# A hybrid decoder layer: storing the split weights of the first down projection for the second, a new order of gate sums and prologue, and another ending

## The chip, the core and the metric

The kernel runs on one core of a Trainium2 chip. The metric is the device time in microseconds (us) of the whole program; lower is better. The core has five engines that run their own instruction streams and meet at semaphores: TensorE (PE, matmuls), VectorE (DVE), ScalarE (ACT), GpSimd (POOL) and SyncE (SP), which here only issues DMA transfers.

## The reference

The input `x` has 2048 tokens of 1024 channels, fp32. There is one layer, and then a final RMSNorm:

```python
mod = (silu(c) @ ada_w[l] + ada_b[l])[:, None, :]
sh1, sc1, g1, sh2, sc2, g2 = jnp.split(mod, 6, axis=-1)
h = rmsnorm(x, norm1_g[l]) * (1 + sc1) + sh1
x = x + g1 * hybrid_mixer(h, ...)      # w_in, a chunked scan, a spatial gate, w_out
h = rmsnorm(x, norm2_g[l]) * (1 + sc2) + sh2
x = x + g2 * conv_gated_ffn(h, ...)
return rmsnorm(x, final_g)

def conv_gated_ffn(h, w_up, conv_w, conv_b, w_down):
    gate, val = jnp.split(h @ w_up, 2, axis=-1)
    gate = causal_dwconv(gate, conv_w, conv_b)
    return (jax.nn.silu(gate) * val) @ w_down
```

The mixer projects to z, x/B/C, dt, u and v; x/B/C go through a causal convolution of width 4 and a chunked scan (16 heads of 64, state 128); u and v through a spatial gating per chunk of 128 tokens; both results, normalized, through `w_out`. The inner width of the FFN is 2816.

## The kernel before, in words

**Tiles and precision.** The tokens are cut into NB = 4 blocks of 512. Every fp32 product is made from halves: an operand is split into a rounded high part and the remainder (fp32r), and three of the four products of halves are summed in PSUM. One **unit** is a weight tile of 128 x 512 with the 12 matmuls (128x512) that use it. PSUM has eight banks: `main[0..3]`, which collect the projections, and `aux[0..3]` (in the profile mostly `pair`).

**Stages.** `mixer(0)`, `mixer(1)`, `ffn(0)` for blocks 0 and 1, `mixer(2)`, `mixer(3)`, `ffn(1)` for blocks 2 and 3. A mixer has 104 units: 0 to 23 for x/B/C (XBC), 24 to 55 for u and v (UV), 56 to 71 for z (Z), 72 to 103 for the output projection (OUT). An FFN takes two blocks at once and makes seven products instead of eight from sums and differences of quarters: 154 units of the up projection, then 77 of the down projection (7 products of KG = 11, in the order P1, P2, P6, P7, P4, P5, P3). In the profiled execution unit 0 of mixer 0 starts at 46.3 us, mixer 1 at 427.0, the first up at 786.3, the first down at 1221.1, mixer 2 at 1446.7, mixer 3 at 1787.7, the second up at 2128.8, the second down at 2561.4; in mixer 0 unit 88 starts at 373.9.

**Weights.** They pass through a ring of RING = 4 slots. SyncE loads a raw tile (`load`, 256 KB), ScalarE makes its high half (`split`, line 811), GpSimd the low one (`low`, line 696), TensorE uses it. Mixer 0 also stores both halves (`store_split`, 512 KB) in `w_split_scratch`, and a split of mixer 0 waits until the halves that stood in its slot before are stored. Mixers 1 to 3 load the halves ready made (line 401): such a load needs a free slot, and no split. Of the 77 weight tiles of down, 35 (`PRE_J`) are loaded, split and stored in mixers 2 and 3 by `pre_load`, `pre_high`, `pre_low`, `pre_store`, and the second down loads these ready made; the other 42 it splits itself, and the first down splits all 77. The up weights' sums are made in mixer 1 and the first up at the units T_AT (`t_load`, `t_store`).

**SyncE** issues in program order. `beside(b, n)` puts other transfers ahead of unit n's load, each with its own waits: the stores of `h_scratch` by mixer 1, the `x2` loads from n = 89 on, the `xnew` loads at n = 79 to 82, and the gate loads at the units `GATE_AT`. While it waits, no later load is issued.

**adaLN.** `mod` needs c_act @ ada_w. For norm 1, `mod_direct` makes the first `ADA_PE` rows' share as matmuls of one column, and VectorE sums the others (`ada_sum`), after which `mod_column` reduces them on TensorE; `mod_column(1)` does so for norm 2 after unit 15. For the two gates, eight blocks `gate_sums(0..7)` on VectorE use 16 loads `gate_load` (two at each of the eight `GATE_AT` units; the loads at index i wait for the sums of block i-1), and eight matmuls (`gate_mm`, after OUT unit 11, that is unit 83) reduce them; SyncE waits for them before the first `x2` load.

**Transposes.** TensorE transposes normalized tokens (`h_transpose`), `y` in two groups (after OUT units 1 and 7) and, for the next block, `h` in two groups (after OUT units 17 and 23), through `aux`; ScalarE takes the high halves out (`yT_hi`), VectorE the low ones.

**Ending.** In the last products of down, P5 and P3 (units 55 to 76), the right-hand halves of the sum are finished: GpSimd multiplies `y_half` by the gate (`final_step`), VectorE adds it to `x_half` (`add_y`, line 1813), ScalarE squares for the last norm, GpSimd multiplies by the gain (`final_gain`), ScalarE scales, SyncE stores. In the same units VectorE makes `a_lo`, the low half of down's left operand (line 1606), for the coming unit.

## Time and profile before

| | us |
|---|---|
| median of 3 runs of the kernel before | 2797.31 |
| lowest and highest of them | 2796.26 and 2800.71 |
| the profiled execution | 2801.3 |
| its span in the trace | 2799.5 |
| TensorE busy in it | 2713.2 (97%) |
| VectorE busy | 1836.2 (66%) |
| GpSimd busy | 1100.9 (39%) |
| ScalarE busy | 994.8 (36%) |
| DMA, mean over the span | 222 GB/s |

The span is cut into stages by the starts of their first units, given above. A windows row has, for a stretch, its length, the busy time and the number of instructions of each engine, the granted clock of TensorE as a share of the full one, the busy share of the 16 DMA engines and what they moved. A timeline row has the start and the length of a run of like instructions, and in brackets how long the engine stood idle before it and what released it.

### The profile page before, as it was taken

Reading aid. Unit: us, or ns where it says so; the run is one execution under the profiler, and the core shown is the slowest. Engines: PE = TensorE matmul, PEld = TensorE weight load, DVE = VectorE, ACT = ScalarE, POOL = GpSimd, SP = SyncE. Lnnn points to the kernel's source line nnn. Section 1 sums busy time; section 2 is a strip of 40 time slices with the busy share of each in tenths; the row PEclk is TensorE's granted clock in tenths of the full one; section 3 lists DMA queues with packets and bytes.
Section 4 is the critical chain, followed back from the end, with each engine's and each line's share of the span. In section 5 each row is a group of like instructions: output and inputs, shape, how many; then the busy total and the mean of one; then the engine's idle time right before and its main releaser. Section 6 shows DMA issues by size and latency. Waiting matters only on the chain.

```text
span 2799.5 us, 33836 instructions
## 1 busy us (share of the span) xinstructions
PE 2713.2 (97%) x12427; PEld 2214.5 (79%) x12427; DVE 1836.2 (66%) x2589; ACT 994.8 (36%) x1505; POOL 1100.9 (39%) x737
## 2 busy tenths in 40 slices
PE   6999999899999999999999999999999999999997
PEld 6777877678877888877878788888888788887885
DVE  6787955668377566568786565565746754545767
ACT  2544323331153333344535322152224433334333
POOL 3344430555047777644560110001003554444244
PEclk9999999999999999999999999999999999999998
DMA  9678777999755665583448767586675334347545
GB/s 385 228 256 298 254 267 256 345 351 332 261 183 187 208 220 188 185 288 88 162 150 293 235 214 277 179 283 231 220 254 191 122 115 121 127 126 249 180 158 199
DMA packets 262001, 620.49 MB, mean 222 GB/s; under 512 B 26725, under 2 KB 84553, under 8 KB 257739
## 3 DMA queue, kind: packets, MB, share of 16 engines
q1 hardware_dynamic: 261174, 618.08, 64.5%
q8 instruction: 99, 1.62, 0.2%
q14 instruction: 66, 0.54, 0.1%
q10 hardware_dynamic: 662, 0.24, 0.0%
HBM read 466.57 MB, written 151.66 MB: 221 GB/s over the span
## 4 chain that ended last, share of the span: by engine, by line
PE 75%; DVE 8%; DMA 7%; POOL 3%; issue 3%; SPq 2%; ACT 1%; DVEq 0%; ACTq 0%; POOLq 0%
PE main L1956 29%; PE pair L2226 15%; PE main L2226 14%; PE pair L2246 6%; PE main L2246 4%; DMA w_split_scratch<-w_hl 2%; POOL tb L714 2%; PE pair L2093 1%; DMA tb<-in_ff_up_dram 1%; DVE a_lo L1606 1%; DMA t_up_scratch<-tb 1%; POOL w_hl L703 1%; PE pair L2118 1%; DMA w_hl<-w_split_scratch 1%; DVE stats L1167 1%
## 5 line engine op out<-in xcount | busy, mean ns | idle before, releaser
L703 POOL TENSOR_TENSOR w_hl<-w_raw,w_hl 128x512 fp32r<-128x512 f32 x532 | 764.1, 1441 | 904.8 <-ACT w_hl L818 902.8
L818 ACT ACTIVATE w_hl<-w_raw 128x512 fp32r<-128x512 f32 x532 | 332.2, 630 | 802.7 <-PE main L2226 169.3
L1956 PE MATMUL main<-w_hl,h_hi 128*128 128x512 f32 x1536 | 492.3, 401 | 4.8 <-DMA w_hl<-w_split_scratch 4.3
L1956 PEld LDWEIGHTS main<-w_hl,h_hi 128*128 128x128 f32 x1536 | 283.8, 188 | 78.3 <-issue 14.2
L1956 PE MATMUL main<-w_hl,h_lo 128*128 128x512 f32 x768 | 300.2, 391 | 0.0
L751 POOL TENSOR_TENSOR pre_hl<-pre_raw,pre_hl 128x512 fp32r<-128x512 f32 x35 | 53.0, 1518 | 564.2 <-ACT pre_hl L842 564.2
L714 POOL TENSOR_TENSOR tb<-tb,tb 128x512 f32<-128x512 f32 x132 | 209.8, 1590 | 164.8 <-DMA tb<-in_ff_up_dram 160.1
L1956 PE MATMUL main<-h_hi,w_hl 128*128 128x512 f32 x768 | 250.6, 400 | 8.2 <-DMA w_hl<-w_split_scratch 5.8
L1606 DVE TENSOR_TENSOR a_lo<-g,a_hi 128x512 fp32r<-128x512 f32 x132 | 176.8, 1349 | 103.4 <-ACT a_hi L1071 103.1
L2226 PE MATMUL pair<-s_hi,w_hl 128*128 128x512 f32 x736 | 235.6, 393 | 2.4 <-POOL w_hl L703 2.4
L2246 PE MATMUL main<-w_hl,a_hi 128*128 128x512 f32 x704 | 222.1, 397 | 16.1 <-DVE a_lo L1606 12.9
L2226 PE MATMUL main<-s_hi,w_hl 128*128 128x512 f32 x672 | 215.5, 393 | 1.9 <-DVE s_lo L1599 1.2
L1669 DVE SCALAR_TENSOR_TENSOR c_acc<-c_gate,col_b,c_acc 128x512 f32<-128x512 f32 x176 | 211.5, 1241 | 4.7 <-ACT c_acc L1037 2.4
L1956 PEld LDWEIGHTS main<-h_hi,w_hl 128*128 128x128 f32 x768 | 146.9, 191 | 41.4 <-DMA w_hl<-w_split_scratch 7.5
L2246 PEld LDWEIGHTS main<-w_hl,a_hi 128*128 128x128 f32 x704 | 132.1, 190 | 52.0 <-issue 17.7
L1956 PEld LDWEIGHTS main<-w_hl,h_lo 128*128 128x128 f32 x768 | 144.1, 188 | 31.7
L2226 PEld LDWEIGHTS pair<-s_hi,w_hl 128*128 128x128 f32 x736 | 138.1, 188 | 35.6 <-POOL w_hl L703 3.2
L2246 PE MATMUL pair<-w_hl,a_hi 128*128 128x512 f32 x528 | 163.3, 390 | 1.4 <-DVE a_lo L1606 1.3
L1956 PE MATMUL main<-w_hl,gmT_hi 128*128 128x512 f32 x512 | 158.5, 391 | 2.2 <-ACT stage L899 1.4
L2226 PEld LDWEIGHTS main<-s_hi,w_hl 128*128 128x128 f32 x672 | 126.1, 188 | 33.5 <-issue 2.9
L1956 PE MATMUL main<-h_lo,w_hl 128*128 128x512 f32 x384 | 151.7, 395 | 0.0
L1956 PE MATMUL main<-w_hl,yT_hi 128*128 128x512 f32 x480 | 150.3, 395 | 0.0
(281 smaller groups left out, 5115.8 us busy)
## 6 DMA issues: line engine op xcount, KB each, us to landing
w_hl<-w_split_scratch SPq DMA_DIRECT2D x312, 512.0 KB, 4.4
w_split_scratch<-w_hl SPq DMA_DIRECT2D x104, 512.0 KB, 6.7
w_raw<-t_up_scratch SPq DMA_DIRECT2D x176, 256.0 KB, 2.7
w_raw<-in_ff_up_dram SPq DMA_DIRECT2D x132, 256.0 KB, 3.7
tb<-in_ff_up_dram SPq DMA_DIRECT2D x88, 256.0 KB, 4.7
t_up_scratch<-tb SPq DMA_DIRECT2D x88, 256.0 KB, 5.7
g_scratch<-c_val SPq DMA_DIRECT2D x44, 512.0 KB, 4.0
g<-g_scratch SPq DMA_DIRECT2D x40, 512.0 KB, 7.3
```

The costliest lines, as they stand in the source:

```text
L703: nc.gpsimd.tensor_tensor(w_lo[:, g % RING, :], w_raw[:, g % RING, :], w_hi[:, g % RING, :].bitcast(F32), ALU.subtract).then_inc(w_lo_ok, 1)
L714: nc.gpsimd.tensor_tensor(dst, one, other, how).then_inc(t_add, 1)
L751: nc.gpsimd.tensor_tensor(pre_hl[i % PRE_BUF][:, 1, :], pre_raw[i % 2][:], pre_hl[i % PRE_BUF][:, 0, :].bitcast(F32), ALU.subtract).then_i ...
L818: nc.scalar.activation(w_hi[:, g % RING, :], w_raw[:, g % RING, :], ACT.Copy).then_inc(w_hi_ok, 1)
L1167: last = V.bn_stats(stats[:, s, :], part)
L1606: V.tensor_tensor(a_lo[j % RING][:], full_a, a_hi[j % RING][:].bitcast(F32), ALU.subtract).then_inc(a_lo_ok, 1)
L1669: last = V.scalar_tensor_tensor(out=piece, in0=c_gate[q % 2][:, i, lo:lo + BT], scalar=col_b[:, R_FW + tap * KF + m:R_FW + tap * KF + m + ...
L1956: ins = T.matmul(main[i], a, w, start=first and p == 0, stop=last and p == 2)
L2093: last = T.matmul(aux[2 + h // (NH // 2)][:, o:o + HD], arow[:, h, :], xdt[:, h * HD:(h + 1) * HD], start=True, stop=True)
L2118: last = T.matmul(aux[2 * (t % 2) + h // 4][:, (h % 4) * P:(h % 4 + 1) * P], wsT[:, h, :], v_sb[:, h // 4, t, (h % 4) * P:(h % 4 + 1) * P] ...
L2226: ins = T.matmul(got[:, i, :], w[:, kl, cols], a[:, k, :], start=k == 0 and m == 0, stop=k == KH - 1 and m == 2)
L2246: ins = T.matmul((main, aux)[p % 2][i], a, w[:, s_w, :], start=k == 0 and m == 0, stop=k == KG - 1 and m == 2)
```

## The change

It has five parts.

**Down's halves.** The first down stores the halves of all its 77 tiles (`store_half(j)`, 512 KB each, issued behind the load of unit j + 4, the last four after the loop), its splits wait until the halves of four units before are stored, and mixer 2's first four loads wait for the last of these stores. The second down loads all 77. Nothing is split in mixers 2 and 3: the four `pre_` functions are gone.

**Prologue.** `mod_direct` goes into `main[1]` in two halves; the transposes of `xn` come between them, ahead of those of the parameter rows, which go to `main[0]`. ScalarE scales `xn` before it copies the parameter columns. `mod_columns` takes its base from a sum made once. The count of `mod_col` is one higher everywhere.

**Mixer 0.** `mod_column(1)` moves from after unit 15 to after unit 18. `GATE_AT` changes; `gate_sums(4)` comes after the scaling of v, 5 after `y_ok`, 6 before and 7 after `norm_x`. The gate matmuls move from after unit 83 to after unit 87. The evacuation of OUT's left half stands ahead of the last split of the loop. The second group of `h` transposes comes two units later, and VectorE makes the first four low halves of `h` ahead of the residual.

**Mixer 1.** `T_AT` starts at unit 20, not 16.

**Ending of the second down.** The gate and gain rows and block 3's `x2` are loaded in P4 into the region of `h` (`g2_last`, `fg_last`, `x_last`). The multiplications of GpSimd are made by VectorE (`gate_half`, `gain_left`, `right_scale`); squares are placed anew; ScalarE scales the left halves (`output_end`).

The diff, cut to its core, eight columns of indentation taken off (a line "..." stands where lines are left out):

```diff
-PRE_J = list(range(2 * KG, 3 * KG + 1)) + list(range(5 * KG - 1, ND))
-pre_d = nc.dram_tensor("down_split_scratch", [len(PRE_J), P, 2, W], F32, kind="Internal").ap()
+pre_d = nc.dram_tensor("down_split_scratch", [ND, P, 2, W], F32, kind="Internal").ap()
 gg_d = nc.dram_tensor("g_scratch", [KF, P, FT], F32, kind="Internal").ap()
...
-GATE_AT = (20, 34, 42, 50, 58, 68, 78, 84)
-PRE_OF = {2: range(17), 3: range(17, len(PRE_J))}
-PRE_AT = [22 + 17 * i // 5 for i in range(18)]
-PRE_BUF = 3
-pre_hi_ok, half_sum, sq_ok = sem("pre_hi_ok"), sem("half_sum"), sem("sq_ok")
+GATE_AT = (22, 34, 42, 50, 58, 70, 80, 85)
+half_sum, sq_ok = sem("half_sum"), sem("sq_ok")
 T_OF = (range(0), range(0, 20), range(20, 33))
-T_AT = ((), [16 + 16 * i // 5 for i in range(20)], [18 + 19 * i // 2 for i in range(13)])
+T_AT = ((), [20 + 16 * i // 5 for i in range(20)], [18 + 19 * i // 2 for i in range(13)])
...
+def half_stored(j):
+    return 16 * (MU // RING) + 16 * (j // RING + 1)
...
+PRE_G = {ffn0(NSB - 1) + DOWN + j: j for j in range(ND)}
+def x_of(s, half):
+    return x_last if half and s == NSB - 1 else x_half[half]
...
+                sp.wait_ge(hl_st[n], half_stored(ND - RING + (n + 1) % RING))
             sp.wait_ge(w_used, mix0(b) + n + 1)
...
-        sp.wait_ge(mod_col, 3)
+        sp.wait_ge(mod_col, 4)
...
+        if s == NSB - 1:
+            sp.wait_ge(half_sum, 4 + (0 if half else 2 * NT) + t + 1)
+        sp.dma_start(ov[2 * s + half, t], x_of(s, half)[:, t, :]).then_inc(y_stored, 16)
+    def store_half(j):
+        g = ffn0(0) + DOWN + j
+        sp.wait_ge(w_lo_ok, split_no(g) + 1 + RING)
+        sp.dma_start(pre_d[j], w_hl[:, g % RING, :, :].bitcast(F32)).then_inc(hl_st[g % RING], 16)
...
-            if (p, k) == (P5, 2):
+            if s + 1 == NSB and p == P4 and 3 <= k < 7:
+                if k == 3:
+                    sp.wait_ge(a_lo_ok, s * ND + (P7 + 1) * KG)
+                    sp.dma_start(g2_last[:], gate_d[1:2, :].broadcast_to([P, D])).then_inc(g2y_in, 16)
+                    sp.dma_start(fg_last[:], final_g.unsqueeze(0).broadcast_to([P, D])).then_inc(fg_in, 16)
+                sp.dma_start(x_last[:, k - 3, :], x2_d[2 * s + 1, k - 3]).then_inc(fin2_in, 16)
+            if s + 1 < NSB and (p, k) == (P5, 2):
...
+                if k == 3:
+                    sp.wait_ge(a_lo_ok, s * ND + (P4 + 1) * KG)
...
+            if s == 0 and j >= RING:
+                store_half(j - RING)
...
+        if s == 0:
+            for j in range(ND - RING, ND):
+                store_half(j)
...
-        pool.wait_ge(d_add, s * (12 + NT) + {(0, 0): 2, (1, 0): 8, (1, 1): 10, (0, 1): 12}[half, c])
+        pool.wait_ge(d_add, s * (12 + NT) + {(0, 0): 2, (1, 0): 8, (1, 1): 10}[half, c])
...
-        if b == NB:
-            for i in range(len(PRE_J)):
-                pre_low(i)
...
-        if b == NB:
-            for step in range(8):
-                final_step(s, step)
-            final_gain(s)
...
-    act.wait_ge(col_tr, 2)
-    nc.scalar.activation(col_a[:], aux[0][:, 0:ROWS_A], ACT.Copy).then_inc(col_ok, 1)
-    nc.scalar.activation(col_b[:], aux[0][:, P:P + ROWS_B], ACT.Copy).then_inc(col_ok, 1)
...
         tile = xn01[:, t, :] if t < 2 else xn23[:, t - 2, :]
         nc.scalar.activation(tile, tile, ACT.Copy, scale=rstd[:, t:t + 1]).then_inc(xn_ok, 1)
+    act.wait_ge(col_tr, 2)
+    nc.scalar.activation(col_a[:], main[0][:, 0:ROWS_A], ACT.Copy).then_inc(col_ok, 1)
+    nc.scalar.activation(col_b[:], main[0][:, P:P + ROWS_B], ACT.Copy).then_inc(col_ok, 1)
...
+        if RING <= g - ffn0(0) - DOWN <= ND:
+            act.wait_ge(hl_st[g % RING], half_stored(g - ffn0(0) - DOWN - RING))
...
-    def half1_scale():
...
+    def left_scale(half, done):
+        for t in range(NT):
+            xx = x_of(NSB - 1, half)[:, t, 0:W]
+            nc.scalar.activation(xx, xx, ACT.Copy, scale=rstd[:, 4 * half + t:4 * half + t + 1]).then_inc(done, 1)
+    def output_end():
         act.wait_ge(r1_ok, 1)
+        left_scale(1, y2_ok)
         for t in range(NT):
-            act.wait_ge(fg_mul, 5 + t // 2)
-            nc.scalar.activation(x_half[1][:, t, :], x_half[1][:, t, :], ACT.Copy, scale=rstd[:, 4 + t:5 + t]
-                                 ).then_inc(y2_ok, 1)
-    def half0_end():
-        for t in range(NT):
-            squares(0, 1, 4 + t + 1, (t,))
+            squares(0, 1, 4 + NT + t + 1, (t,))
         act.wait_ge(xr_ok, NSB + 1)
-        for t in range(NT):
-            nc.scalar.activation(x_half[0][:, t, 0:W], x_half[0][:, t, 0:W], ACT.Copy, scale=rstd[:, t:t + 1]
-                                 ).then_inc(y20_ok, 1)
+        left_scale(0, y20_ok)
...
+                if j == 0 and n == n0 + 2 * KD + LEAD - 1:
+                    evac_to_stage(G_OUT, S_OUT, n0 + 2 * KD - 1, ACT.Copy)
...
-                if b % 2 == 0 and j == 1 and n in (n0 + LEAD + 1, n0 + LEAD + 7):
+                if b % 2 == 0 and j == 1 and n in (n0 + LEAD + 1, n0 + LEAD + 9):
...
-            if j == 0:
-                evac_to_stage(G_OUT, S_OUT, n0 + 2 * KD - 1, ACT.Copy)
...
+            if s == NSB - 1 and p == P5 and k in (6, 7):
+                squares(1, 0, 1, (2 * k - 12, 2 * k - 11))
             if s == NSB - 1 and p == P5 and k in (9, 10):
-                squares(0, 0, 1, (2 * k - 18, 2 * k - 17))
-            if s == NSB - 1 and p == P3 and k in (6, 7):
-                squares(1, 0, 2, (2 * k - 12, 2 * k - 11))
-            if (s, p, k) == (NSB - 1, P3, 8):
-                squares(1, 1, 3)
+                squares(0, 0, 2, (2 * k - 18, 2 * k - 17))
+            if s == NSB - 1 and p == P3 and k in (7, 8):
+                squares(1, 1, 3, (2 * k - 14, 2 * k - 13))
...
+        dve.wait_ge(mod_col, done + 1)
+        cols = two_parts(mod_c, 2 * n * KD, ks)
+        link(V.tensor_tensor(cols, two_parts(bank, 0, ks), base, ALU.add))
         V.scalar_tensor_tensor(out=cols[:, 1, :], in0=cols[:, 1, :], scalar=1.0,
...
+    dve.wait_ge(mod_col, 1)
+    link(V.tensor_tensor(mod_c[:, 0:2 * KD], main[1][:, 0:2 * KD], col_b[:, R_AB:R_AB + 2 * KD], ALU.add))
...
-        mod_columns(0, slice(4 * half, 4 * half + 4), (main[3 - 2 * half], main[2]), R_N1, 1 + half)
-    dve.sem_inc(evacuated, 4)
-    full_at = [acc[:, 0, :], acc[:, 1, :]]
-    h_lows(0, (0, 1), aux, full_at)
+        ks = slice(4 * half, 4 * half + 4)
+        mod_columns(0, ks, main[3 - half], two_parts(mod_c, 0, ks), R_N1, 1 + half)
+        dve.sem_inc(evacuated, 2)
+        if half == 0:
+            h_lows(0, (0, 1), aux, full_at)
...
-                mod_columns(1, slice(0, KD), (aux[0],), R_N2, 3)
+                mod_columns(1, slice(0, KD), aux[0], two_parts(col_b, R_AB + 2 * KD, slice(0, KD)), R_N2, 3)
...
-            if b == 0:
+            if b == 0 and cc < NT - 1:
...
+        if b == 0:
+            gate_sums(NT)
...
-        if b == 0:
-            gate_sums(5)
...
-            gate_sums(6)
+            gate_sums(5)
...
-            gate_sums(7)
+            gate_sums(6)
...
+            gate_sums(7)
...
+        if b == 0:
+            h_lows(b + 1, range(4), aux, [acc[:, 0, :], acc[:, 1, :]])
...
-            h_lows(b + 1, range(KD), aux, [acc[:, 0, :], acc[:, 1, :]])
+            h_lows(b + 1, range(0 if b else 4, KD), aux, [acc[:, 0, :], acc[:, 1, :]])
...
-            if (p, k) == (P5, 7):
-                dve.wait_ge(pool_fin, s * 6 + 2)
-                add_y(s, 0, 0)
...
+                if (p, k) == (P5, 1):
+                    gate_half(s, 0, 0, 2)
+                if (p, k) == (P5, 4):
+                    gate_half(s, 1, 0, 8)
+                if (p, k) == (P5, 5):
+                    add_y(s, 1, 0)
+                if (p, k) == (P5, 8):
+                    add_y(s, 0, 0)
+                if (p, k) == (P5, 10):
+                    gain_left(s, 1, NT)
+                if (p, k) == (P3, 1):
+                    gain_left(s, 0, 2 * NT)
                 if (p, k) == (P3, 5):
-                    dve.wait_ge(pool_fin, s * 6 + 4)
-                    add_y(s, 1, 0)
+                    gate_half(s, 1, 1, 10)
+                if (p, k) == (P3, 6):
+                    add_y(s, 1, 1)
                 if (p, k) == (P3, 7):
-                    dve.wait_ge(pool_fin, s * 6 + 6)
-                    add_y(s, 1, 1)
+                    gate_half(s, 0, 1, 12)
                 if (p, k) == (P3, 8):
-                    dve.wait_ge(pool_fin, s * 6 + 8)
                     add_y(s, 0, 1)
         if s == NSB - 1:
             dve.wait_ge(sq_ok, 3 * NT)
             rms_rstd(NT, r1_ok, 4, True)
+            dve.wait_ge(r1_ok, 1)
+            right_scale(1)
...
+    def gate_half(s, half, c, after):
+        cols = slice(c * W, (c + 1) * W)
+        dve.wait_ge(g2y_in, 16 * (s + 1))
+        dve.wait_ge(d_add, s * (12 + NT) + after)
+        yy = y_half[half][:, :, cols]
+        link(V.tensor_tensor(yy, yy, g2_last[:, cols].unsqueeze(1).broadcast_to([P, NT, W]), ALU.mult))
+    def gain_left(s, half, squared):
+        dve.wait_ge(fg_in, 16 * (s + 1))
+        dve.wait_ge(sq_ok, squared)
+        xx = x_of(s, half)[:, :, 0:W]
+        link(V.tensor_tensor(xx, xx, fg_last[:, 0:W].unsqueeze(1).broadcast_to([P, NT, W]), ALU.mult))
...
-    mod_direct(main[2])
-    pe.wait_ge(rows_in, 176)
-    T.transpose(aux[0][:, 0:ROWS_A], rows_a[0:ROWS_A, :], ident[0:ROWS_A, 0:ROWS_A]).then_inc(col_tr, 1)
-    T.transpose(aux[0][:, P:P + ROWS_B], rows_b[0:ROWS_B, :], ident[0:ROWS_B, 0:ROWS_B]).then_inc(col_tr, 1)
-    pe.wait_ge(col_ok, 2)
+    mod_direct(main[1], range(KD))
     pe.wait_ge(xn_ok, NT)
     h_transpose(0, range(4), xn, aux)
+    pe.wait_ge(rows_in, 176)
+    T.transpose(main[0][:, 0:ROWS_A], rows_a[0:ROWS_A, :], ident[0:ROWS_A, 0:ROWS_A]).then_inc(col_tr, 1)
+    T.transpose(main[0][:, P:P + ROWS_B], rows_b[0:ROWS_B, :], ident[0:ROWS_B, 0:ROWS_B]).then_inc(col_tr, 1)
+    mod_direct(main[1], range(KD, 2 * KD)).then_inc(mod_col, 1)
...
-    mod_column(0, range(4, KD), main[1])
+    mod_column(0, range(4, KD), main[2])
...
-                if b == 0 and (j, k) == (1, 7):
+                if b == 0 and (j, k) == (2, 2):
...
-                if b == 0 and j == 0 and k == 11:
+                if b == 0 and j == 0 and k == 15:
...
-                if b % 2 == 0 and j == 1 and k in (1, 7):
+                if b % 2 == 0 and j == 1 and k in (1, 9):
```

## Rows read from the trace of the kernel before

**Rows 1.** Windows of core 0: mixer 0, mixer 1, first down, mixer 2, second down.

```profile
core 0: us, PE busy (x) PEld busy (x) DVE busy (x) ACT busy (x) POOL busy (x), PEclk, DMA share, GB/s
46.30:427.00 380.70, 365.69 (x1716) 295.41 (x1717) 288.28 (x457) 151.58 (x234) 160.58 (x102) 0.97 0.74 268
427.00:786.30 359.30, 346.78 (x1654) 281.73 (x1653) 223.73 (x403) 94.07 (x132) 128.09 (x82) 1.00 0.88 311
1221.10:1446.70 225.60, 217.91 (x958) 175.38 (x958) 174.98 (x176) 103.86 (x172) 136.66 (x89) 1.00 0.50 167
1446.70:1787.70 341.00, 341.00 (x1653) 281.63 (x1652) 221.54 (x452) 95.51 (x139) 26.30 (x17) 1.00 0.71 241
2561.40:2799.50 238.10, 215.67 (x925) 175.11 (x923) 167.42 (x179) 85.80 (x155) 97.25 (x53) 0.96 0.57 200
```

**Rows 2.** Chain of waits: start us, length us, engine, line, count.

```profile
721.14 54.43 PE main L1956 x240
```

**Rows 3.** Waits of TensorE: total us, times, longest us.

```profile
PE main L2246 <- DVE a_lo L1606: 12.9, 13, 4.2
```

**Rows 4.** Timeline, PE: start us, length us, instruction [idle before, releaser].

```profile
33.63 3.65 PE L1903 MATMUL pair<-ident,xn 128*128 128x128 f32 x16 [4.74 <-ACT xn L808]
```

**Rows 5.** Timeline, ScalarE, before unit 8.

```profile
70.13 0.63 ACT L818 ACTIVATE w_hl<-w_raw 128x512 fp32r<-128x512 f32 x1 [0.95 <-DMA w_split_scratch<-w_hl]
```

**Rows 6.** The ending: timelines of TensorE and VectorE, and a window.

```profile
2770.56 1.19 PE L2246 MATMUL main<-w_hl,a_hi 128*128 128x512 f32 x2 [4.17 <-DVE a_lo L1606]
...
2725.92 2.29 DVE L1813 TENSOR_TENSOR x_half<-x_half,y_half 128x2048 f32<-128x2048 f32 x1
...
2763.16 4.49 DVE L1813 TENSOR_TENSOR x_half<-x_half,y_half 128x2048 f32<-128x2048 f32 x1
...
2743.40:2786.90 43.50, 35.15 (x133) 26.88 (x131) 41.77 (x33) 14.37 (x29) 32.32 (x10) 0.88 0.46 170
```

**Rows 7.** Window after the column matmuls of norm 2.

```profile
108.00:114.00 6.00, 6.00 (x16) 4.80 (x16) 5.34 (x9) 3.41 (x5) 1.48 (x1) 0.50 0.69 186
```

**Rows 8.** Timeline, PE: the column matmuls of norm 2.

```profile
101.52 6.98 PE L1914 MATMUL pair<-tri,mod_sum 128*128 128x1 f32 x32 [3.47 <-DVE mod_sum L1225]
```

**Rows 9.** Timeline, VectorE: two blocks of gate sums.

```profile
319.68 2.47 DVE L1235 SCALAR_TENSOR_TENSOR mod_sum<-mod_sum,c_act 128x1024 f32<-128x1024 f32 x2
...
340.16 3.50 DVE L1235 SCALAR_TENSOR_TENSOR mod_sum<-mod_sum,c_act 128x1024 f32<-128x1024 f32 x2
```

**Rows 10.** Timeline, SyncE's DMA issues: a gate load, the first `x2` load.

```profile
321.06 1.50 SPq L437 DMA_DIRECT2D mod_sum<-in_ada_w_dram  x2
...
361.46 0.33 SPq L544 DMA_DIRECT2D x<-in_x_dram  x1
```

**Rows 11.** Timeline, ScalarE: splits 78 and 89, `yT_hi`, an evacuation.

```profile
330.55 0.63 ACT L818 ACTIVATE w_hl<-w_raw 128x512 fp32r<-128x512 f32 x1 [4.68 <-DMA w_split_scratch<-w_hl]
...
340.99 2.42 ACT L996 ACTIVATE yT_hi<-pair,col_a 128x512 fp32r<-128x512 f32 x4 [0.38 <-PE pair L2140]
...
368.11 0.63 ACT L818 ACTIVATE w_hl<-w_raw 128x512 fp32r<-128x512 f32 x1 [3.02 <-DMA w_split_scratch<-w_hl]
...
373.19 2.04 ACT L899 ACTIVATE stage<-main 128x512 f32<-128x512 f32 x4
```

**Rows 12.** Timeline, PE: second `y` transposes, gate matmuls.

```profile
344.86 2.15 PE L2140 MATMUL pair<-ident,y_sb 128*128 128x128 f32 x16
...
357.84 3.59 PE L2179 MATMUL pair<-mod_sum,tri 128*1 128x512 f32 x8
```

**Rows 13.** Window in mixer 1.

```profile
480.00:530.00 50.00, 40.46 (x169) 31.19 (x168) 31.15 (x39) 17.56 (x25) 24.16 (x17) 0.97 0.98 355
```

**Rows 14.** Two windows in the first down projection.

```profile
1221.00:1262.00 41.00, 39.84 (x175) 32.37 (x174) 27.06 (x27) 16.83 (x29) 19.81 (x15) 1.00 0.94 342
...
1232.00:1242.00 10.00, 9.30 (x42) 7.40 (x41) 5.45 (x4) 4.02 (x8) 4.84 (x4) 1.00 1.04 391
```

**Rows 15.** Timeline, SyncE: mixer 2's first loads.

```profile
1438.91 20.13 SPq L401 DMA_DIRECT2D w_hl<-w_split_scratch  x7
```

**Rows 16.** The page's DMA issues: KB each, median us to landing.

```profile
w_hl<-w_split_scratch SPq DMA_DIRECT2D x312, 512.0 KB, 4.4
```

113 lines of the change are left out of this document (29 added, 84 removed).

## The prediction

> **What bounds the kernel now.** I read the stretches first. TensorE is busy 346.78 of 359.30 us in mixer 1, 217.91 of 225.60 in the first down projection, 341.00 of 341.00 in mixer 2 and 215.67 of 238.10 in the second down with the ending [rows 1]. The chain of waits gives its pace: 240 matmuls in 54.43 us, so a unit of 12 takes 2.72 us [rows 2], and 77 down units need 209.4 us. So only time in which TensorE stands still, or runs at the half clock, can be won. The largest wait of it is for `a_lo` from VectorE, 12.9 us [rows 3]; the reader should see that mixers 2 and 3, where the change takes 35 splits away, have no such time. What is left: idle time in the prologue, mixer 0, mixer 1 and at the end; and the new waits, which come from SyncE's queue, where every load stands behind everything issued or waited for before it.
>
> **1. Prologue, about +2.4 us.** Transposing `xn` before the parameter rows removes the 4.74 us wait in front of them [rows 4]; with half of `mod_direct` (its columns 8 to 15) also behind the transposes, I let unit 0 start 6.8 us earlier, near 39.5 instead of 46.3. But unit 8 needs ScalarE to evacuate `main`, and that is queued behind the split at 70.13, which waits for the store of an earlier split and takes 0.63 [rows 5]. The transfer queue has the same bytes in the same order until then. So unit 8 still starts at 70.76 + 0.5 for the first bank = 71.3, the 6.8 us is lost again, and TensorE stands about 6 us before it. In the ending, where it stood 4.17 us, it was granted 0.88 over 43.5 us [rows 6], and in 108 to 114 it got 0.50, which is 1.2 GHz, after standing for the column sums [rows 7, 8]. Bounds: 0 to +2.7 for the clock (one unit at half speed costs its 2.72 again), −3 if the queue moves; I take +2.4.
>
> **2. First part of mixer 0, −1.9.** The column matmuls of norm 2 waited 3.47 us for VectorE's sums, after unit 15 [rows 8]. Moved to after unit 18 they don't, but the `da_t` transposes after unit 17 now come 3 us before VectorE has them (its chain is unchanged), and the half clock comes later: −0.9. VectorE reaches the convolutions with less waiting, −1.0 (0 to −1.8).
>
> **3. Gate sums, mixer 0's second half, +12.5.** Here SyncE gets two new blocks.
> (a) `gate_sums(4)` goes behind the scaling of `v_sb` (−2.5 for TensorE), `gate_sums(5)`, 2.47 us at 319.68, behind `y_ok`. `y_ok` is reached where the next gate sum starts, 340.2; without one block of 2.5 ahead and the other it comes at 340.2 − 2.5 − 2.4 = 335.3 [rows 9]. But gate load 6, now at n = 80, waits for `gate_sums(5)`: release at 335.3 + 1.4 = 336.7. Before, the same wait stood at n = 78 and ended at 321.06 [rows 10], and split 78 then started at 330.55, 9.5 us later [rows 11]. With one more `xnew` load ahead, split 80 comes at 346 and split 81, by the 3.1 us pace of such a full queue, at 349.3. ScalarE's `yT_hi` is behind split 81 (before: 340.99 [rows 11]), so 350; its VectorE residues and the second group of `y` transposes end at 354. Before, that group started at 344.86 and took 2.15 [rows 12], so unit 80 began at 347; without the block VectorE's 2.5 us would bring the group to 342.4. Now unit 80 begins at 354 + 0.2: +7.2, and +2.4 for the clock after 11 us of standing.
> (b) The gate matmuls go from after unit 83 to after unit 87. They ended at 357.84 + 3.59 = 361.4 [rows 12] and SyncE, which had waited for them before the first `x2` load at n = 89, went on at 361.46 [rows 10]; four more units were then in the ring. Now only unit 88 is. Loads 89 ff. stand behind the wait; split 89 started at 368.11, 6.65 us after release, and only after it comes the evacuation (373.19 before [rows 11]) that unit 88 needs. The evacuation is moved ahead of split 90, not of split 89. Unit 80 at 354.2, eight units of 2.72 and the 2.2 of the last group give 378.0 for the gate matmuls, 381.6 for their end; unit 88 waits 8 us behind it (6.65 and the split, then the first bank) and starts at 389.6 against 373.9, +15.7, which holds the +7.2 of (a); the clock is again 2.4. The second group of `h` transposes, two units later, no longer waits for `h_lo`, which VectorE now makes earlier: I put 5.9 on that and on the units at half clock behind it that go. 15.7 + 2.4 − 5.9 = 12.2 and 0.3 for the longer wait of the `x2` loads: **+12.5** (bounds: +5, if the blocks overlap and the clock stays; +17).
>
> **4. Mixer 1, −3.** It takes 359.3 against 341.0 of mixer 2, and most of the difference lies in 480 to 530, where TensorE is busy 40.5 of 50 at 355 GB/s [rows 1, 13]. Shifting `T_AT` by four units separates its first transfers from the four `h_scratch` stores (2 MB, at 391 GB/s about 5 us) but puts another 1.2 rounds into the fast units at the end, each some 2.5 us. Bounds −9 to +1.
>
> **5. First down, +8.5; its end, +2.2.** It moves 342 GB/s × 41 us = 14.0 MB in 1221 to 1262, and the queue is full at 391 GB/s [rows 14]. By unit 19 (1221.1 + 19 × 2.72, and 1.8 of waits: 1274.6), 16 stores of 0.52 MB join: with the loads of units up to 19 some 22.4 MB / 390 GB/s = 57.5 us, to 1279, and 2.2 us for latency and 2.1 for split and subtraction: unit 19 at 1283.1 instead of 1274.6. Each split waits for the store of the unit four before, so this is a bound, not a backlog. After unit 19 a unit moves 0.79 MB, 2.0 us: hidden. Bounds: +4 (latency overlaps) to +11. At the end SyncE must store unit 76, which begins at 1446.7 − 2.72 and whose split is ready only a little before, I say 1443.7, before it loads mixer 2's unit 0. It issued that load at 1438.9 [rows 15] and needed it at 1446.7. At 1444.2 and with a median landing of 4.4 us [rows 16] it lands at 1448.6, and 0.3 for the store ahead: +2.2 (0 to +5). Taking 17 pre-splits out of mixer 2 and 18 out of mixer 3 costs and gives nothing there; its cover was slack on all three engines.
>
> **6. Second down, −1.0 up to its last units.** No splits: some of the short waits for them and for VectorE in the first units go. Loaded units may be issued only when the slot is free, three units (8.2 us) ahead, instead of seven. With one 0.52 MB piece of `g` per unit, units 4 to 19 ask for 1.05 MB / 2.72 us = 386 GB/s, just under the 391 seen: I take +0.5 of stall (0 to +4) and −1.5 from the splits.
> The Trainium skill speaks against this part: "DMA: Bandwidth & Descriptors", Specifications, gives about 358 GB/s of HBM as a core's limit, by which the load here would outrun the queue; its page "Perfetto Trace Analysis", Engine Utilization, says that a core alone can draw more, up to some 435. The trace agrees with the second, 391 [rows 14], so the sum doesn't use the first.
>
> **7. Ending, −12.9.** In the last units three additions to `x_half` take 4.49 us each beside GpSimd's multiplications, where one alone took 2.29; TensorE waits for VectorE, 4.17 us at most, and is granted 0.88. The last product's 11 units took 43.5 us, from 2743.4 to 2786.9 [rows 6]; unstalled they take 29.9: 13.6. The change takes the gate and gain multiplications to VectorE: in each step from unit 68 on it gets 2.3 (a multiplication like the lone addition) + 0.7 = 3.0 us, over the pace of 2.72, but it starts three units ahead and stays 4 us ahead. VectorE still has the right half of half 1 (4 × 0.7) when the banks fill; the tail after TensorE is 0.9 (up to 2) longer. −13.6 + 0.9 = −12.7, and −0.2 for shorter output stores: −12.9 (−9 to −15).
>
> **Sum.** 2.4 − 1.9 + 12.5 − 3 + 8.5 + 2.2 − 1.0 − 12.9 = **+6.8 us**. The profiled execution took 2801.3 us (span 2799.5 and 1.8 around it), so 2808.1 for its like; it lies 4.0 above the median of 2797.3, so the median becomes **2804.1**, 0.24% slower.
>
> **Rivals.**
> A, not slower: SyncE's block at n = 80 is hidden. It decides at unit 80: if VectorE ends the gate sums by 327 there (ten us before my time), the loads come in time, 9.6 us of term 3 are gone, and the time is 2804.1 − 9.6 = 2794.5, or 2797 with term 1 as it is and the block half hidden. For it: VectorE had waits in that stretch. Against: the wait at n = 78 was seen to delay the splits by 9.5 us.
> B, the stores of the first down are hidden, as they are in mixer 0, which moves 268 GB/s [rows 1] with hardly a wait: term 5 falls to +2, total 2797.6. Against: the 391 GB/s.
> C, the second down starves. Its loads have 8.2 us, not 19. Where a round of transfers outruns 2.72 us per unit, 0.3 us × 15 units and first misses of 3 us are lost, and each standstill costs clock: 2812. The queue rate at which that begins is 386 GB/s. The Trainium skill's 358 GB/s ("DMA: Bandwidth & Descriptors", Specifications), if it held, would do this by itself: 2.93 us per unit there, and 5.1 us more in the first down, about 2812.
> D, the ending gains little, since VectorE, now with the multiplications, is late at unit 74: 4 us ahead becomes none if an addition still takes 4.5; then −6, total 2811. Against: GpSimd has no work left there.
>
> **How the numbers follow.** Forecast (2799 to 2809 by itself) 0.42; A 0.19; B 0.14; C 0.15; D 0.10. A measurement of this kernel can tell 0.2%, 5.6 us, from no change: 2791.7 to 2802.9. Of the forecast's 0.42, 0.17 lies below 2802.9; of A 0.12 lies below 2791.7 (mixer 1 gains up to its 9 us too) and 0.07 within; of B 0.03 below and 0.11 within. Faster 0.12 + 0.03 = 0.15; same 0.17 + 0.07 + 0.11 = 0.35; slower 0.25 + 0.15 + 0.10 = 0.50. The range reaches from A's 2794.5 less some of mixer 1's bound, 2791, to 2815, past C and D.
>
> **What would show it.** Unit 8 near 71.3 in spite of an early unit 0; SyncE released near 337 and splits 80 and 81 after 345; unit 88 some 8 us after the gate matmuls; unit 19 of the first down 8 to 9 us late, with 390 GB/s; a mixer 2 whose first unit waits; no `a_lo` wait over 1 us at the end. Mixer 0 not longer than before, or a first down under 228 us, would make the prediction wrong.

## The result

The changed kernel takes 2824.59 us (median of 4 runs, 2823.3 to 2824.86) against 2799.01 (4 runs): ratio 1.0091, interval [1.0078, 1.0103], +25.6 us. The forecast was 2804.1, +6.8 us, and its range ended at 2815. The profiled execution took 2824.86 us.

Windows of the changed kernel, by stage as [rows 1] (mixer 0, mixer 1, first down, mixer 2, second down with the ending), then the last product's 11 units as the window in [rows 6]:

```profile
39.00:441.90 402.90, 366.13 (x1717) 296.02 (x1718) 293.78 (x459) 151.32 (x234) 158.06 (x102) 0.95 0.72 260
441.90:800.00 358.10, 346.09 (x1654) 281.86 (x1653) 218.80 (x405) 94.48 (x132) 125.42 (x82) 1.00 0.89 312
1235.00:1482.90 247.90, 224.01 (x958) 175.14 (x956) 173.85 (x178) 104.16 (x172) 137.77 (x89) 0.99 0.86 314
1482.90:1825.60 342.70, 342.70 (x1652) 282.85 (x1653) 213.81 (x450) 85.91 (x122) 0.00 (x0) 1.00 0.59 201
2599.10:2823.10 224.00, 210.24 (x925) 173.11 (x923) 133.37 (x186) 64.31 (x116) 0.00 (x0) 0.98 0.73 260
...
2780.40:2810.50 30.10, 30.10 (x134) 24.69 (x132) 26.77 (x38) 11.53 (x24) 0.00 (x0) 1.00 0.60 208
```

To be seen against [rows 1]: the first down grew from 225.6 to 247.9 us with the same work of TensorE, at 314 GB/s instead of 167. Mixer 0 ends 14.9 us later (441.9 against 427.0). Mixer 1 is 1.2 shorter, mixer 2 1.7 longer. The second down lost 14.1 us, nearly all in its last product, 30.1 us instead of 43.5 and at the full clock. GpSimd has nothing to do in mixer 2 (x0). 14.9 − 1.2 + 22.3 + 1.7 − 14.1 = 23.6, the spans' difference. The forecast had 6.8 for the same sum; of the 16.8 us between them 13.3 lie in the first down and the start of mixer 2.

Mixer 0's two standstills, in the timelines of SyncE, ScalarE and TensorE (start, length, instruction, idle time before it and its releaser), as [rows 10 to 12] had them:

```profile
337.28 1.52 SPq L433 DMA_DIRECT2D mod_sum<-in_ada_w_dram  x2
...
347.93 0.63 ACT L789 ACTIVATE w_hl<-w_raw 128x512 fp32r<-128x512 f32 x1 [17.21 <-DMA w_split_scratch<-w_hl]
351.06 0.63 ACT L789 ACTIVATE w_hl<-w_raw 128x512 fp32r<-128x512 f32 x1 [2.51 <-DMA w_split_scratch<-w_hl]
351.60 2.40 ACT L951 ACTIVATE yT_hi<-pair,col_a 128x512 fp32r<-128x512 f32 x4
...
353.11 3.68 PE L2124 MATMUL pair<-ident,y_sb 128*128 128x128 f32 x16 [10.47 <-DVE yT_lo L1472]
...
380.61 3.59 PE L2163 MATMUL pair<-mod_sum,tri 128*1 128x512 f32 x8
...
390.89 0.63 ACT L789 ACTIVATE w_hl<-w_raw 128x512 fp32r<-128x512 f32 x1 [14.82 <-DMA w_split_scratch<-w_hl]
391.42 2.04 ACT L857 ACTIVATE stage<-main 128x512 f32<-128x512 f32 x4
...
392.15 1.19 PE L1940 MATMUL main<-w_hl,gmT_hi 128*128 128x512 f32 x2 [7.95 <-ACT stage L857]
```

SyncE was released at 337.28 (forecast 336.7). Splits 80 and 81 came at 347.9 and 351.1 (346 and 349.3), `yT_hi` right behind (350), so the second `y` transposes stood 10.5 us. The gate matmuls ended at 384.2 (381.6); split 89 came 6.7 us later (6.65) and unit 88 at 392.15 (389.6).

The first down's unit 4 in the changed kernel, timelines of ScalarE, VectorE and TensorE, and a window from the end of unit 7 to unit 17:

```profile
1247.37 0.63 ACT L789 ACTIVATE w_hl<-w_raw 128x512 fp32r<-128x512 f32 x1 [2.54 <-DMA down_split_scratch<-w_hl]
...
1248.55 1.34 DVE L1561 TENSOR_TENSOR a_lo<-g,a_hi 128x512 fp32r<-128x512 f32 x1 [5.96 <-ACT a_hi L1023]
...
1250.03 0.70 PE L2230 MATMUL main<-w_hl,a_hi 128*128 128x512 f32 x2 [3.20 <-DVE a_lo L1561]
...
1262.00:1297.00 35.00, 29.24 (x119) 21.20 (x118) 18.32 (x18) 14.51 (x24) 13.87 (x11) 1.00 1.04 410
```

The split of unit 5 waits for the store of unit 1; `a_hi` of unit 4 is behind it on ScalarE, `a_lo` behind that, and TensorE stands 3.2 us. Then the queue moves 410 GB/s and TensorE is busy 29.2 of 35 us. The Trainium skill ("DMA: Bandwidth & Descriptors", Specifications) puts the ceiling of the DMA fabric at 435 GB/s and HBM's share of a core at 358; this window lies between, so the second does not bind here.

### The profile page after: what moved, and what is told of

It reads as the page before. It is cut to its first block, busy times and chain, and to the rows that moved or that the text cites. A ratio compares the mean times of both kernels' runs of the same rounds, so it can differ in the third digit from the quotient of the medians.

```text
span 2823.1 us, 33569 instructions
## 1 busy us (share of the span) xinstructions
PE 2712.5 (96%) x12427; PEld 2211.3 (78%) x12427; DVE 1785.7 (63%) x2598; ACT 952.9 (34%) x1428; POOL 941.9 (33%) x646
## 4 chain that ended last, share of the span: by engine, by line
PE 73%; DVE 8%; DMA 7%; issue 3%; POOL 3%; SPq 2%; ACT 1%; DVEq 0%; ACTq 0%; POOLq 0%
PE main L1940 29%; PE pair L2210 14%; PE main L2210 14%; PE main L2230 5%; PE pair L2230 4%; DMA w_split_scratch<-w_hl 3%; PE pair L2077 2%; POOL w_hl L695 2%; DMA down_split_scratch<-w_hl 1%; PE pair L2102 1%; POOL tb L706 1%; DMA t_up_scratch<-tb 1%; DVE a_lo L1561 1%; DMA tb<-in_ff_up_dram 1%; DVE stats L1118 1%
## 5 line engine op out<-in xcount | busy, mean ns | idle before, releaser
L695 POOL TENSOR_TENSOR w_hl<-w_raw,w_hl 128x512 fp32r<-128x512 f32 x490 | 704.5, 1442 | 1462.0 <-ACT w_hl L789 1450.1
L789 ACT ACTIVATE w_hl<-w_raw 128x512 fp32r<-128x512 f32 x490 | 306.4, 630 | 800.0 <-PE main L2210 178.9
L1940 PEld LDWEIGHTS main<-w_hl,h_hi 128*128 128x128 f32 x1536 | 284.7, 189 | 82.3 <-issue 17.4
L1940 PE MATMUL main<-h_hi,w_hl 128*128 128x512 f32 x768 | 252.6, 403 | 11.5 <-ACT stage L857 5.5
L1561 DVE TENSOR_TENSOR a_lo<-g,a_hi 128x512 fp32r<-128x512 f32 x132 | 132.3, 1009 | 144.5 <-ACT a_hi L1023 143.8
L2210 PE MATMUL pair<-s_lo,w_hl 128*128 128x512 f32 x368 | 144.6, 393 | 0.0
```

The costliest lines, as they stand in the source:

```text
L695: nc.gpsimd.tensor_tensor(w_lo[:, g % RING, :], w_raw[:, g % RING, :], w_hi[:, g % RING, :].bitcast(F32), ALU.subtract).then_inc(w_lo_ok, 1)
L789: nc.scalar.activation(w_hi[:, g % RING, :], w_raw[:, g % RING, :], ACT.Copy).then_inc(w_hi_ok, 1)
L1561: V.tensor_tensor(a_lo[j % RING][:], full_a, a_hi[j % RING][:].bitcast(F32), ALU.subtract).then_inc(a_lo_ok, 1)
L1940: ins = T.matmul(main[i], a, w, start=first and p == 0, stop=last and p == 2)
L2210: ins = T.matmul(got[:, i, :], w[:, kl, cols], a[:, k, :], start=k == 0 and m == 0, stop=k == KH - 1 and m == 2)
```

## The experiments

The parts of the change are named: **stored halves**; **prologue** with the later column matmuls of norm 2; **gates** (gate sums, gate loads, gate matmuls); **h/evacuation** (the later `h` transposes, the early low halves, the evacuation's place); **T_AT**; **ending**. Differences in us are ratios times 2800. A stage's length in an experiment is taken from the starts of its first units in the trace.

### Each part alone

`a_only` is the kernel before with the stored halves alone, `not_a` the changed kernel without them.

> The kernel before with one part of the change alone: the first down projection stores all 77 halves, the second loads them, nothing is split in mixers 2 and 3. My theory after the two traces (each part costs what the stretch in which it lies shows): the first down 22 us longer (225.6 to about 248), the first two units of mixer 2 another 2 us, the second down within 1 us: about +24 us, ratio 1.0085. Rival (the first down is long because the work reaches it in another rhythm after mixer 0's new standstills, and the stores are mostly hidden, as forecast): +8 to +11 us, ratio 1.003 to 1.004.

Measured: 1.0086 [1.0071, 1.0101], +24.1 us; in the trace the first down holds 21.8 of it. Mixer 2's start is only 0.1 us later here, while it lost 1.7 in the changed kernel.

> The changed kernel without that part: the halves of 35 tiles are made in mixers 2 and 3 as before; prologue, mixer 0, mixer 1 and ending are the changed ones. My theory: mixer 0 14.9 us longer than before, mixer 1 1.2 shorter, the ending 13.6 shorter, first down as before: within 1 us of the kernel before, ratio 1.000. Rival (the parts depend on each other): it differs from the kernel before by more than 4 us.

Measured: 1.0015 [1.0005, 1.0024], +4.2 us (1.4 to 6.7), not the 0 expected, and at the edge of what the rival said. In the trace mixer 0 ends 12.9 us later (14.9 said) and the last product is 13.4 shorter (13.6 said), but mixer 1 took 3.5 us more, where the changed kernel, with the same code there, took 1.2 less. This lies within the spread of mixer 1's length, given below under `t_only`, and doesn't show that the parts depend on each other.

> The kernel before with the new ending of the second down alone. My theory: the last eleven units lose their waits for VectorE: -13.6 us, ratio 0.9951, and no wait for a_lo over 1 us in them. Rival (part of the gain comes from the loaded halves, which free GpSimd and VectorE of the splits in the second down): -9 us or less, ratio 0.997.

Measured: 0.9949 [0.9934, 0.9964], −14.3 us. The last product takes 30 us (the window below begins 0.3 us after its first matmul), and no wait for `a_lo` in the second down is over 0.4 us; the waits of TensorE in it (total, times, longest) and the product's window:

```profile
PE main L2270 <- POOL w_hl L717: 0.5, 1, 0.5
PE main L2270 <- DVE a_lo L1602: 0.4, 1, 0.4
...
2738.00:2767.70 29.70, 29.70 (x132) 24.31 (x130) 26.83 (x38) 11.46 (x24) 0.00 (x0) 1.00 0.60 207
```

> The kernel before with the new order of gate sums, gate loads and gate matmuls, the evacuation ahead of the last split and the later h transposes alone. My theory: SyncE's two blocks cost mixer 0 some 15 us (unit 80 +10 us, unit 88 +18), ratio 1.0053. Rival (the standstills come from the changed prologue, whose transfers crowd later): +5 us or less, ratio under 1.002.

Measured: 1.0054 [1.0037, 1.007], +15.1 us, with the gates and h/evacuation.

The five parts alone (the two others follow below: 1.1 and 3.6) add up to 24.1 − 14.3 + 15.1 + 1.1 + 3.6 = 29.6 us, against 25.6 for all together; each has an interval of 2.5 to 4.6 us to both sides, so this is no sign of a dependence. The stored halves cost 24.1 us where the forecast had 9.7 (steps 5 and 6). These 14.4 us are most of the miss of 18.8, not all of it.

### Where the first down loses

`a_first`, on top of `a_only`:

```diff
-                    split(f0 + DOWN + j + LEAD)
+                    if s:
+                        split(f0 + DOWN + j + LEAD)
                     if 4 <= j + 2 < ND:
                         a_high(j + 2)
+                    if s == 0:
+                        split(f0 + DOWN + j + LEAD)
```

> The kernel with the stored halves alone (the part that cost 24 us), and in the first down ScalarE makes the high half of down's left operand (a_hi) ahead of the split of the step, not behind it. Theory 1 (the splits stand on ScalarE until an old half is stored, and a_hi, a_lo and TensorE stand behind them): the waits for a_lo from unit 9 on go, some 12 of the 22 us; what is left is the full transfer queue up to unit 19, 8 to 11 us: total about +11 us against the kernel before. Theory 2 (the bytes of the stores alone set the pace): no change against the stored halves alone, +24 us.

Measured: 1.0076 [1.006, 1.0093], +21.3 us. Theory 1 falls. The two intervals overlap, so the time alone doesn't even show the 3 us; in the traces the first down is 4.3 us shorter than `a_only`'s (243.0 against 247.3), and 1.6 of that come back at the start of mixer 2. The order on ScalarE is worth some 3 us, not 12.

`half_store`, on top of `a_only`:

```diff
-sp.dma_start(pre_d[j], w_hl[:, g % RING, :, :].bitcast(F32))
+sp.dma_start(pre_d[j][:, :, 0:W // 2], w_hl[:, g % RING, :, 0:W // 2].bitcast(F32))
```

and the second down loads `hl_d` in the place of `pre_d`.

> The kernel with the stored halves alone, but each store has half the bytes (256 of 512 columns), with the same issues and waits; the second down loads other stored halves instead of down's, so its products are not the layer's, and its transfers are of the same size. Theory 1 (order on ScalarE and the latency of a store): the early stall shrinks from 11 to about 3 us, since a unit then moves 1.05 MB, but later splits still wait: +10 to +14 us in the first down. Theory 2 (bytes): under +4 us.

Measured: 1.0036 [1.0021, 1.0051], +10.1 us. Theory 2 falls: with half the bytes the stage still loses 9.9 us. That lies at the lower end of theory 1, of which `a_first` had refuted the order, so that the wait for a store's landing is left of it. About half of the loss (11.9 of 21.8 us) goes with half the bytes. The share of the bytes may be larger, since half the bytes are not half the work of the queue: this kernel has 272863 packets, 104377 of them under 2 KB, where `a_only` has 263007 and 84665.

`late_store`, on top of `a_only`: `PRE_G` holds units 20 to 76, `store_half` starts at j = 24, and splits before unit 24 wait for no store.

> The kernel with the stored halves alone, but only the tiles of units 20 to 76 are stored and loaded; the second down splits the first 20 itself. If the stall up to unit 19 is the transfers of g and stores together, those 14 us go and the 8 us behind unit 20 stay: about +9 us against the kernel before. Rival (the stall is a price per store, wherever it stands): three quarters of 24 us, +18.

Measured: 1.0024 [1.001, 1.0037], +6.7 us. The rival's +18 falls; in the trace the 14.3 us up to unit 20 are gone (0.4 is left).

`mid_store`: as `late_store`, but stores of units 20 to 51 only, and the second down loads the later ones from `hl_d`.

> As the kernel that stores from unit 20 on, but only units 20 to 51 are stored; the second down loads units 52 to 76 from other stored halves, so its products there are not the layer's, and its transfers are of the same size. Theory: the late 8 us lie at units 56, 57 and 70 to 74, where ScalarE scales x_next (4.3 us) or makes h tiles and the splits behind it can't catch up, because each waits for a store: without stores there, the first down is as before, total within 2 us of the kernel before. Rival (each store costs a little, wherever it stands): 32 of 57 stores, +4 us.

Measured: 1.0002 [0.9993, 1.0012], +0.6 us. The rival's +4 lies just outside the interval (−2.0 to +3.4); in the trace the stage is 226.1 us long, 0.5 more than before.

The first down in windows, up to unit 20 and from there to mixer 2. In order: `a_only`, `a_first`, `half_store`, `late_store`, `mid_store`, and the kernel before:

```profile
1222.10:1292.60 70.50, 60.48 (x241) 45.76 (x240) 39.20 (x39) 25.71 (x43) 28.65 (x21) 0.95 0.99 378
1292.60:1469.50 176.90, 166.62 (x717) 132.67 (x717) 132.51 (x138) 78.39 (x130) 108.87 (x69) 0.98 0.82 289
```
```profile
1225.30:1293.80 68.50, 59.48 (x242) 45.10 (x240) 39.55 (x39) 25.93 (x43) 29.09 (x21) 0.98 1.01 384
1293.80:1468.30 174.50, 165.46 (x717) 131.48 (x717) 133.13 (x140) 78.72 (x129) 107.64 (x69) 0.99 0.82 296
```
```profile
1215.20:1276.20 61.00, 55.50 (x242) 44.66 (x240) 39.59 (x39) 25.39 (x43) 28.53 (x20) 1.00 0.99 349
1276.20:1450.60 174.40, 162.95 (x717) 130.46 (x717) 139.06 (x140) 78.60 (x131) 108.79 (x69) 1.00 0.62 209
```
```profile
1217.10:1273.70 56.60, 54.97 (x241) 44.89 (x240) 39.50 (x40) 24.68 (x41) 28.11 (x20) 1.00 0.80 288
1273.70:1450.30 176.60, 166.55 (x717) 132.46 (x715) 132.21 (x138) 79.32 (x131) 108.68 (x69) 0.98 0.81 289
```
```profile
1223.80:1280.30 56.50, 55.00 (x241) 44.89 (x240) 39.49 (x40) 24.73 (x41) 28.09 (x20) 1.00 0.81 289
1280.30:1449.90 169.60, 162.84 (x717) 130.46 (x716) 134.98 (x137) 79.43 (x131) 108.65 (x69) 1.00 0.65 225
```
```profile
1221.10:1277.30 56.20, 55.04 (x242) 44.91 (x242) 39.56 (x40) 24.68 (x41) 28.03 (x20) 1.00 0.77 276
1277.30:1446.70 169.40, 162.87 (x718) 130.47 (x717) 135.41 (x137) 79.17 (x131) 108.63 (x69) 1.00 0.41 131
```

Read as lengths. Up to unit 20: 70.5, 68.5, 61.0, 56.6, 56.5, before 56.2. Where the stores run beside the loads of `g`, the DMA share is 0.99 and the stretch is 14.3 us longer; half the bytes take two thirds of that away, later stores all of it. Behind unit 20: 176.9, 174.5, 174.4, 176.6, 169.6, before 169.4. Here the mean DMA share is 0.82 and TensorE still loses 7.5 us; without the stores of units 52 to 76 it loses none, and with all stores at half the bytes it still loses 5.0. What happens there, in ScalarE's and TensorE's timelines of `late_store`:

```profile
1369.56 0.63 ACT L790 ACTIVATE w_hl<-w_raw 128x512 fp32r<-128x512 f32 x1 [1.57 <-issue]
1370.09 0.61 ACT L1027 ACTIVATE a_hi<-g 128x512 fp32r<-128x512 f32 x1
1370.62 4.25 ACT L1078 ACTIVATE x_next<-x_next,rstd 128x1024 f32<-128x1024 f32 x4
1377.83 0.63 ACT L790 ACTIVATE w_hl<-w_raw 128x512 fp32r<-128x512 f32 x1 [2.96 <-DMA down_split_scratch<-w_hl]
1378.36 0.61 ACT L1027 ACTIVATE a_hi<-g 128x512 fp32r<-128x512 f32 x1
1380.98 0.63 ACT L790 ACTIVATE w_hl<-w_raw 128x512 fp32r<-128x512 f32 x1 [2.01 <-DMA down_split_scratch<-w_hl]
...
1380.49 0.82 PE L2202 MATMUL pair<-w_hl,a_hi 128*128 128x512 f32 x2 [2.86 <-DVE a_lo L1562]
```

ScalarE scales `x_next` for 4.25 us and is late. In the kernel before it then caught up, a split every 1.96 us, waiting only for loads:

```profile
1379.40 0.63 ACT L818 ACTIVATE w_hl<-w_raw 128x512 fp32r<-128x512 f32 x1 [0.95 <-DMA w_raw<-t_down_scratch]
1379.94 0.61 ACT L1071 ACTIVATE a_hi<-g 128x512 fp32r<-128x512 f32 x1
1381.35 0.63 ACT L818 ACTIVATE w_hl<-w_raw 128x512 fp32r<-128x512 f32 x1 [0.80 <-DMA w_raw<-t_down_scratch]
```

With the stores it waits 2.96 us for one and goes on at 3.15 us a split, slower than TensorE's 2.72, so `a_hi` is late for the next ones too. The mean of 0.82 hides why the wait is so long. SyncE had issued no store for 10 us, from 1361.1 to 1371.5, and then issues stores, raw tiles and the four pieces of `x_half` (2 MB) in one burst. The queue is full: a store landed about 4 us after its issue before the burst, 10.1 us after it in the burst. Windows of `late_store` and, at the same place, of the kernel before, which fills its queue there too, but whose splits wait for no store (TensorE stands 0.90 us instead of 2.86):

```profile
1378.00:1385.00 7.00, 4.51 (x13) 3.60 (x14) 2.69 (x2) 2.99 (x6) 2.70 (x3) 0.76 1.03 417
```
```profile
1380.00:1386.00 6.00, 5.10 (x23) 3.92 (x22) 4.23 (x4) 3.58 (x8) 3.89 (x4) 1.00 1.04 410
```

Units 55 to 64 hold 4.1 of the 7.2 us that `late_store` loses behind unit 20. `a_first` takes the jump at units 56 and 57 away, and others come at 71 and 72: the lateness is moved, not removed, as long as the splits themselves wait. No run keeps the stores and takes only the splits' wait away, or gives the ring more slots, so that the price of the wait by itself is argued from `half_store`, `mid_store` and these rows, not measured.

### Mixer 0

`mm15` is h/evacuation with the gate matmuls behind unit 87, the gate sums as before:

```diff
-if b == 0 and j == 0 and k == 11:
+if b == 0 and j == 0 and k == 15:
```

> The kernel before with the gate matmuls behind unit 87 instead of 83, the evacuation ahead of the last split and the later h transposes; gate sums and gate loads as before. It has SyncE's second block alone. Theory: unit 80 as before; the gate matmuls end at 368.7 + 3.6 = 372.3, unit 88 starts 8 us later at 380 to 381 and TensorE then has the half clock for a unit, +9; the h transposes give 6 back: +3 us, so the first block (unit 80) is the remaining 11 of the 14.3 us. Rival (the two blocks feed each other): 0 or less.

Measured: 1.0018 [1.0008, 1.0028], +5.0 us, unit 88 at 380.76.

`hv_only` is h/evacuation alone.

> The kernel before with two small edits of mixer 0's end alone: the second group of h transposes two units later (with the first four low halves of h ahead of the residual), and the evacuation of OUT's left half ahead of the last split. In every kernel with them TensorE's standstill before unit 96 and the half clock behind it were gone, 6 us by unit 98. Theory: that gain needs nothing else of the change, -6 us, ratio 0.998. Rival (it only gives back what the block at unit 88 had cost, VectorE being ahead because TensorE stood): 0.

Measured: 0.9979 [0.9968, 0.999], −5.9 us. TensorE's windows about units 94 to 97 of `hv_only` and of the kernel before:

```profile
390.00:401.00 11.00, 11.00 (x58) 9.31 (x57) 6.72 (x9) 2.87 (x5) 5.33 (x4) 1.00 0.97 347
```
```profile
399.00:410.00 11.00, 9.40 (x33) 7.37 (x34) 8.80 (x13) 3.64 (x6) 2.54 (x2) 0.69 0.39 133
```

Before, the `h` transposes waited for `h_lo` three times (0.8, 0.8 and 0.7 us), and the granted clock fell to a mean of 0.69 over the 11 us, with 0.50, that is 1.2 instead of 2.4 GHz, from 402 to 405. So by differences: gate matmuls 5.0 + 5.9 = 10.9 us, gate sums and loads 15.1 − 5.0 = 10.1, h/evacuation −5.9. Each of these times has an interval of 3 to 5 us to both sides, but the traces say the same at the place. From unit 78 to the start of mixer 1 the nine kernels with the old code there take 87.9 to 91.2 us (mean 88.9), `hv_only` and `ehv` 83.2 and 83.4, `mm15` 93.4 and `gates_only` 104.7: −5.6, then +10.2, then +11.3.

`evac_early`, gates and h/evacuation with the evacuation one step earlier:

```diff
-if j == 0 and n == n0 + 2 * KD + LEAD - 1:
+if j == 0 and n == n0 + 2 * KD + LEAD - 2:
```

> As the new order of gate sums and gate matmuls alone (14.3 us slower than before), but with the evacuation one step earlier, ahead of split 89. Theory: unit 88 no longer waits for split 89, whose tile SyncE issues only behind the gate matmuls, but unit 89 still does: unit 88 starts right behind the gate matmuls, and some 3 us of the 10 come back, +11 us against the kernel before. Rival (unit 88 waited for something else, VectorE's rows or the bank): +14 us.

Measured: 1.0032 [1.0019, 1.0046], +9.0 us (15.1 without the step, the intervals overlap). In the traces unit 88 starts 8.0 us sooner behind unit 87, unit 89 gives back 4.6 and unit 90 1.4: some 2 us of gain are shown at the place, where TensorE now waits for the tile that was issued late:

```profile
391.75 1.22 PE L1958 MATMUL main<-w_hl,gmT_hi 128*128 128x512 f32 x2 [5.72 <-POOL w_hl L703]
```

### The rest, and a faster kernel

> The kernel before with the changed prologue and the later column matmuls of norm 2 alone. As forecast: unit 0 early, unit 8 at 71 to 72, unit 9 behind a half clock, the standstill before unit 16 gone and one before units 18 and 19 in its place: +0.5 us (-2 to +3), no difference that can be measured. Rival (the gain of unit 16 stays): -5 us.

Measured: 1.0004 [0.9995, 1.0013], +1.1 us. The rival falls: by unit 18 it was 8.4 us ahead of the kernel before, by unit 24 1.0.

> The kernel before with the transfers of the up weights' sums in mixer 1 four units later, alone. Forecast -3 us (-9 to +1); in the kernels with all other parts mixer 1 took 1.2 us less or 3.5 us more than before, so that I now expect -1 to +2 us, and between units 19 and 31 the standstills shifted, not removed. Rival (they are removed): -6 us or more.

Measured: 1.0013 [1.0002, 1.0023], +3.6 us. From unit 19 to 29 it gains 5.7 us on the kernel before, at units 30 and 31, where TensorE waits 1.40 and 1.70 us for loads, it loses 4.3, and from unit 31 to 79 another 7.2. How much of this is the change shows against the spread of single executions: the thirteen kernels with the old `T_AT` take 38.5 to 42.4 us from unit 19 to 29, the three with the new one 34.7 to 35.2; then 7.3 to 7.5 against 9.5 to 11.6 up to unit 31; then 176.9 to 183.0 against 181.2 to 186.9 up to unit 79. Mixer 1 as a whole takes 356.9 to 363.8 against 358.1 to 364.6. The gain and the loss at units 30 and 31 are clear; the later loss is not separated from the spread.

> The kernel before with the two parts that gained, the new ending and the edits of mixer 0's end. Theory (the parts add up): -14 - 6 = -20 us, near 2780 us, ratio 0.993. Rival (only the ending counts): -14 us, ratio 0.995.

`ehv` has the ending and h/evacuation. Measured: 2782.18 us (5 runs), 0.9938 [0.9924, 0.9951], −17.4 us: faster than both kernels. The interval holds both −20 and −14; that both parts gain is seen in its trace, 83.4 us from unit 78 to mixer 1 and 30.1 us for the last product.

## Why the prediction was wrong

Per step, forecast, measured with the part alone, and in the trace of the changed kernel:

| step | forecast | alone | from | in the changed kernel |
|---|---|---|---|---|
| 1, 2 prologue, norm 2 | +0.5 | +1.1 | `pm_only` | |
| 3 (a) block at unit 80 | +9.6 | +10.1 | `gates_only` less `mm15` | |
| 3 (b) block at unit 88 | +8.8 | +10.9 | `mm15` less `hv_only` | |
| 3 `h` transposes | −5.9 | −5.9 | `hv_only` | steps 1 to 3: +14.9 |
| 4 mixer 1 | −3 | +3.6 | `t_only` | −1.2 |
| 5 first down and mixer 2's start | +10.7 | +21.9 | trace of `a_only` | +24.0 |
| 6 second down up to its last product | −1.0 | +0.1 | trace of `a_only` | −0.6 |
| 7 ending | −12.9 | −14.3 | `end_only` | −13.5 |

(3 (b) is 15.7 + 2.4 + 0.3 less the 9.6 of (a).) The last column adds up to 23.6, the forecasts to 6.8. Step 5 alone is 13.3 of the difference, steps 1 to 3 are 1.9 and step 4 is 1.8.

**Step 5 failed**: it forecast +8.5 us for the first down, which took 22.3 more. It did so in three places.

First, "unit 19 at 1283.1", 8.5 us late. It came out 12.6 us late, 66.0 us after the stage began (62.0 forecast, 53.4 before). The bytes were right: the 16th store had landed after 60.2 us (57.5 and 2.2 for latency, 59.7, were forecast). But I let only the tile's own split and subtraction follow, and unit 19 waited for neither. The last standstill lay before unit 17. ScalarE splits unit j + 3 before it makes `a_hi` of unit j + 2, so that the store that releases one unit's split also holds the operand of the unit before it. The 15th store landed after 57.7 us and released the split of unit 18, and `a_hi` and `a_lo` of unit 17 stood behind it, 2.8 us up to TensorE; units 17 and 18 then took 5.5:

```profile
1292.80 0.63 ACT L789 ACTIVATE w_hl<-w_raw 128x512 fp32r<-128x512 f32 x1 [1.19 <-DMA down_split_scratch<-w_hl]
...
1295.49 0.70 PE L2230 MATMUL pair<-w_hl,a_hi 128*128 128x512 f32 x2 [1.16 <-DVE a_lo L1561]
```

`a_first`, without this order, has unit 19 3.0 us earlier than `a_only` (63.5 against 66.6 after the stage's start), and unit 20 2.0 earlier. Term 5 also had nothing for the clock, which terms 1 and 3 did count: behind its standstill unit 4 took 4.4 us (5.3 in `a_only`) instead of 2.8.

Second, "after unit 19 a unit moves 0.79 MB: hidden". The mean was right (289 GB/s), the reading of it wrong: it asked for bytes and not for the chain, nor for where the bytes fall. A split that must wait for the landing of a store of four units before can't run ahead, and what it ran ahead by was what had covered ScalarE's 4.25 us of other work; and just there SyncE's burst fills the queue, and a store takes 10.1 us to land. 7.5 us, at a mean DMA share of 0.82.

Third, the bounds. "Bounds: +4 to +11" had their upper end from the same argument as the value, so that the range could not hold an error in it. [Rows 11] had, in mixer 0, splits with 3.02 and 4.68 us of idle time before them for a store, in the same construction: the row to take a bound from. 3 us for each of the three places at which TensorE stood (3.20 us before unit 4, 3.07 before 8, 2.95 before 56) would have given 9 us more.

**Step 4** had the wrong sign for the part alone: I priced the transfers that moved away and "1.2 rounds" that moved in, at 2.5 us each, but called the first larger without a row. The gain is there (5.7 us), and more is lost (11.5); only the 4.3 at units 30 and 31 of that are traced to waits for loads. In a stage whose length varies by up to 6.9 us between kernels with the same code there, its exact share in the changed kernel (1.2 us shorter there) stays open.

**Steps 1 to 3, 6 and 7 held.** SyncE's release and splits 80, 81 and 89 came out within 3 us, and so did units 8 (71.0, forecast 71.3), 80 (356.4, forecast 354.2) and 88, because each was counted from a row of the same wait elsewhere. That some terms agree to a few tenths is luck: the intervals of the times alone are wider. In step 7 the last product gained 13.4 us (13.6 forecast), but the 0.9 us for a longer tail did not come: the tail is 0.1 shorter. Rival A (the block hidden) is refuted by the 10.47 us before the `y` transposes, B (the stores hidden as in mixer 0) and its price of 2 by `a_only`; C did not occur, TensorE waits 1.3 us for loaded halves in the second down; nor D. None of the rivals had the first down lose more than forecast: this was the one missing.

## What to carry over

A store that must land before a ring slot is filled again can cost twice, as bytes in the queue and as lost lead of the engine that refills. Ask of each engine how much it runs ahead, what irregular work lives on this lead, and who is queued behind the wait. "Hidden on average" is no answer: look for the place where the issuing engine has paused and then issues a burst. When a part is moved in a queue that is full, look at the units to which its bytes go as carefully as at those they leave; and give a range's upper end another argument than its middle.

## What the runs showed of the hardware

The DMA queue reached 410 GB/s over 35 us with loads and stores mixed, above the 391 in [rows 14]; so the forecast's 390 was not too high, and the loss did not come from the rate.

The clock did not answer to equal standstills in an equal way. In the first 70.5 us of `a_only`'s first down it was 0.95, where the kernel before and the one with late stores have 1.00: TensorE had stood 4.79 us before unit 4, and in the 4 us behind that it was granted 0.50, the lower level. Before unit 56 it stood 2.93 us in `a_only` and 2.95 in the changed kernel; in the 4 us behind, the first was granted 0.62 and the second 1.00:

```profile
1400.16:1404.16 4.00, 4.00 (x11) 3.14 (x12) 1.36 (x1) 1.52 (x3) 1.28 (x1) 0.62 1.03 416
```
```profile
1412.47:1416.47 4.00, 3.79 (x16) 2.85 (x17) 1.37 (x1) 1.52 (x3) 1.29 (x1) 1.00 1.03 418
```

So a standstill of about 3 us has no fixed price in clock: unit 56 took 4.4 us in `a_only`, 3.2 in the changed kernel and 2.8 in the kernel before.
